# Conditioning sums moved between VectorE and GpSimd, and score matmuls in another order, in a one-core decoder layer

## The reference, cut to what matters

```
mod = silu(c) @ W_ada + b_ada          # 1024 x 6144: shift/scale/gate for both halves
h   = rms_norm(x) * (1 + scale1) + shift1
proj = h @ w_in                        # attention q,k,v; deltanet q,k,v; beta, decay; gates
branch A: window-128 attention, 8 query heads, 2 key heads, head width 64, sinks
branch B: gated delta rule, 4 heads of 128, short causal convolution on its inputs
x   = x + gate1 * ((sigmoid(gA)*(oA @ W_A) + sigmoid(gB)*(oB @ W_B)) @ w_out)
h   = rms_norm(x) * (1 + scale2) + shift2
x   = x + gate2 * ((silu(h @ w_gate) * (h @ w_up)) @ w_down)
```

## Time and profile before

| | us |
|---|---|
| median of 3 runs | 3558.05 (3557.0 to 3559.01) |
| the profiled execution | 3557.41 |
| its span, first to last instruction | 3555.7 |
| busy in the span: TensorE, VectorE, ScalarE, GpSimd | 3389.5, 1803.5, 1180.2, 176.1 |

### The profile page before, as it was taken

One profiled execution on the slowest core, in us unless ns is written; L12 is line 12 of the kernel. 1 busy time (PEld: TensorE's weight loads), 2 busy tenths in 40 slices (PEclk: granted clock), 3 DMA queues, 4 the chain that ended last, 5 costly groups with the idle time before them and its releaser, 6 DMA issues.

```text
span 3555.7 us, 49320 instructions
## 1 busy us (share of the span) xinstructions
PE 3389.5 (95%) x20664; PEld 2970.6 (84%) x20664; DVE 1803.5 (51%) x2806; ACT 1180.2 (33%) x1827; POOL 176.1 (5%) x171
## 2 busy tenths in 40 slices
PE   7999998999999999899999999899999999989999
PEld 7887788889888778798889777889888877788898
DVE  2866564434455565444354565544436465643333
ACT  1343343222233333323233334332223433432222
POOL 2001101000000100100000100000000010010000
PEclk9999999999999999999999999999999999989999
DMA  5430122332331113232232011322323211122222
GB/s 209 173 122 32 36 85 82 101 107 95 125 99 50 33 34 110 81 103 98 97 131 95 31 36 41 109 95 101 101 95 125 77 37 36 59 96 95 95 95 95
DMA packets 87388, 312.65 MB, mean 88 GB/s; under 512 B 10112, under 2 KB 18432, under 8 KB 85504
## 3 DMA queue, kind: packets, MB, share of 16 engines
q1 hardware_dynamic: 78720, 301.12, 25.1%
q10 hardware_dynamic: 8448, 8.39, 0.7%
HBM read 301.09 MB, written 8.39 MB: 87 GB/s over the span
## 4 chain that ended last, share of the span: by engine, by line
PE 85%; DVE 8%; ACT 3%; issue 1%; POOL 1%; DVEq 1%; POOLq 0%; ACTq 0%
PE gb L1306 37%; PE gb L1323 26%; PE gb L1562 5%; PE mb L1516 3%; PE mb L1499 2%; PE gb L1356 2%; PE gb L1251 2%; PE mb L1434 1%; PE mb L1273 1%; POOL d_rs L518 1%; PE mb L1504 1%; PE mb L1459 1%; DVE conv_acc L983 1%; PE mb L1519 1%; DVE d_ss L1085 1%
## 5 line engine op out<-in xcount | busy, mean ns | idle before, releaser
L570 ACT ACTIVATE w_hi<-w_raw 128x1024 fp32r<-128x1024 f32 x492 | 520.3, 1058 | 1258.7 <-PE gb L1306 601.8
L1306 PE MATMUL gb<-h_hi,w_hi 128*128 128x512 f32 x2256 | 891.5, 395 | 2.1 <-DVE w_lo L863 2.1
L863 DVE TENSOR_TENSOR w_lo<-w_raw,w_hi 128x1024 fp32r<-128x1024 f32 x492 | 600.5, 1222 | 576.0 <-ACT w_hi L570 571.3
L1306 PE MATMUL gb<-h_hi,w_lo 128*128 128x512 f32 x2256 | 887.1, 393 | 0.0
L1306 PE MATMUL gb<-h_lo,w_hi 128*128 128x512 f32 x2256 | 883.6, 392 | 0.0
L1306 PEld LDWEIGHTS gb<-h_hi,w_hi 128*128 128x128 f32 x2256 | 424.2, 188 | 87.2 <-DVE w_lo L863 4.2
L1306 PEld LDWEIGHTS gb<-h_hi,w_lo 128*128 128x128 f32 x2256 | 424.1, 188 | 85.1
L1306 PEld LDWEIGHTS gb<-h_lo,w_hi 128*128 128x128 f32 x2256 | 424.1, 188 | 84.7
L1323 PE MATMUL gb<-w_hi,hid_lo 128*128 128x256 f32 x1408 | 398.5, 283 | 0.0
L1323 PE MATMUL gb<-w_lo,hid_hi 128*128 128x256 f32 x1408 | 398.5, 283 | 0.0
L1323 PE MATMUL gb<-w_hi,hid_hi 128*128 128x256 f32 x1408 | 398.4, 283 | 0.0
(11 more groups left out here) (274 smaller groups left out, 4829.3 us busy)
## 6 DMA issues: line engine op xcount, KB each, us to landing
w_raw<-in_wstream SPq DMA_DIRECT2D x492, 512.0 KB, 3.3
ada_buf<-in_ada_w SPq DMA_DIRECT2D x12, 2048.0 KB, 8.0
xs<-in_x SPq DMA_DIRECT2D x16, 512.0 KB, 4.5
x<-in_x SPq DMA_DIRECT2D x4, 2048.0 KB, 8.6
out<-x ACTq DMA_DIRECT2D x16, 512.0 KB, 4.8
bias_row<-in_ada_br SPq DMA_DIRECT2D x1, 1024.0 KB, 11.9
gains<-in_qkg SPq DMA_DIRECT2D x1, 64.0 KB, 12.0
nrm_g<-in_g SPq DMA_DIRECT2D x2, 4.0 KB, 3.8
```

The costliest lines, as they stand in the source:

```text
L570: act.activation(w_hi[s][:, :], w_raw[s][:, :], ACT.Copy).then_inc(w_high.sem, 1)
L863: dve.tensor_tensor(w_lo[s][:, :], w_raw[s][:, :], w_hi[s][:, :].bitcast(fp32), ALU.subtract).then_inc(w_ready.sem, 1)
L1306: last = pe.matmul(bank(j), w, r, start=(i == 0), stop=(i == n - 1))
```

## The change

1. The first four turns go to VectorE (`ada_sums(0..3)`), between the scalings of the first four token tiles. TensorE makes only the sum over partitions. Turns 0 to 3 have buffers of their own, loaded first; the token rows `xs` of tiles 0 and 1 come behind turn 0, turn 3 comes in two halves.
2. Turns 4 to 9 go to GpSimd: it multiplies the whole 128x4096 piece by the vector, then adds halves (2048, 1024 and 512 elements a partition). They stand in its program directly behind the four shifts of the rows.
3. Turns 10 and 11 stay on VectorE, turn 10 behind the small chain on beta and decay, turn 11 in the output gate; they use a fifth buffer. TensorE takes the turns in the order 4, 5, 6, 7, 8, 10, 9, 11. SyncE loads turn 6, 7, 8, 9 ahead of units 9, 12, 15, 18.
4. The angles of the rotary embedding (some 22 small VectorE operations) and the `w_lo` of units 0 and 1 move from VectorE's start to behind the last `h_lo`.
5. The score matmuls alternate between the two halves of the rows, and the products of the probabilities with the values are issued own-own-old-old instead of own-old-own-old.

The core of the diff:

```diff
-ADA_ISSUE = {0: (4, 5), 8: (6,), 11: (7,), 14: (8,), 17: (9,), 20: (10,), 22: (11,)}
+ADA_ISSUE = {0: (4, 5), 4: (10,), 9: (6,), 12: (7,), 15: (8,), 18: (9,), 20: (11,)}
+ADA_ORDER = (0, 1, 2, 3, 4, 5, 6, 7, 8, 10, 9, 11)
+ADA_ON_POOL = (4, 5, 6, 7, 8, 9)
...
+            pool.wait_ge(c_silu, 1)
+            for turn in ADA_ON_POOL:
+                buf = ada_buf[turn % 2]
+                pool.wait_ge(ada_in[turn % 2], 16 * (turn // 2))
+                pool.tensor_tensor(buf[:, :, :], buf[:, :, :], cs[:, :].unsqueeze(2).to_broadcast([P, KD, 512]), ALU.mult)
+                for n in (4, 2):
+                    pool.drain()
+                    pool.tensor_tensor(buf[:, 0:n, :], buf[:, 0:n, :], buf[:, n:2 * n, :], ALU.add)
+                pool.drain()
+                pool.wait_ge(ada_prod, ada_place(turn - 2))
+                pool.tensor_tensor(ada_total(turn), buf[:, 0, :], buf[:, 1, :], ALU.add).then_inc(ada_pooled, 1)
...
-            for t in range(NT):
-                scale_tile(t)
-            split(0, 0)
-            split(0, 1)
             dve.wait_ge(cond_in, 16 * N_COND)
             dve.wait_ge(c_silu, 1)
-            for early in range(ADA_FIRST):
-                modulation(early)
+            ada_sums(0)
+            scale_tile(0)
+            scale_tile(1)
+            ada_sums(1)
+            modulation(0)
+            scale_tile(2)
+            ada_sums(2)
+            modulation(1)
+            scale_tile(3)
+            ada_sums(3)
+            modulation(2)
+            modulation(3)
...
+            norm_low(2, 3, h_hi, h_lo)
+            norm_low(3, 4, h_hi, h_lo)
+            split(0, 0)
+            split(0, 1)
             dve.wait_ge(pos_in, 16)
...
-                    if b == 0 and c in (2, 5, 8, 11):
-                        ada_sums(ADA_FIRST + c // 3)
-                    if b == 0 and c in (9, 11):
-                        modulation(4 + (c - 9) // 2)
+                    if b == 0 and c in (8, 11):
+                        modulation(4 + (c - 8) // 3)
...
-                        for parity in range(2):
-                            rows = slice(64 * parity, 64 * parity + 64)
-                            for old, keys in enumerate((kT[t % 2], kT[(t + 1) % 2])):
-                                for a in range(2):
+                        for old, keys in enumerate((kT[t % 2], kT[(t + 1) % 2])):
+                            for a in range(2):
+                                for parity in range(2):
+                                    rows = slice(64 * parity, 64 * parity + 64)
                                     last = pe.matmul(m(2 * g + parity)[:, 2 * old + a, :], qT[rows, 2 * g + a, :],
                                                      keys[rows, g, :], start=True, stop=True)
```

More of the change, by code:

```diff
@@ L421, in _, with load_piece @@
             sp.dma_start(nrm_g[:, 1, :], g2).then_inc(cond_in, 16)
-            for turn in range(2):
-                sp.dma_start(ada_buf[turn][:, :, :], ada_w[turn]).then_inc(ada_in[turn], 16)
+            def load_piece(turn, k, some=slice(0, KD)):
+                sp.dma_start(ada_buf[k][:, some, :], ada_w[turn][:, some, :]).then_inc(ada_in[k], 16)
+            load_piece(0, 0)
+            for i in range(2):
+                sp.dma_start(xs[:, i, :], x_t[0, :, i, :]).then_inc(xs_loaded[i].sem, 16)
+            load_piece(1, 1)
+            load_piece(2, 2)
+            load_piece(3, 3, slice(0, 4))
+            load_piece(3, 3, slice(4, 8))
             for i in (2, 3):
@@ L426, in _ @@
                 sp.dma_start(xs[:, i % 2, :], x_t[0, :, i, :]).then_inc(xs_loaded[i % 2].sem, 16)
-            for turn in range(2, ADA_FIRST):
-                sp.dma_start(ada_buf[turn][:, :, :], ada_w[turn]).then_inc(ada_in[turn], 16)
+            sp.dma_start(pos_i[:, :], pos).then_inc(pos_in, 16)
             def load_unit(b, u):
@@ L796, in _ @@
             MAGIC = float(1.5 * 2 ** 23)
[L797 to L820, removed]
             def modulation(turn):
                 v, half = divmod(turn, 2)
-                dve.wait_ge(ada_prod, turn + 1)
+                dve.wait_ge(ada_prod, ada_place(turn))
                 if is_gate(turn):
@@ L919, in _ @@
             norm_low(3, 4, h_hi, h_lo)
+            split(0, 0)
+            split(0, 1)
+            dve.wait_ge(pos_in, 16)
+            dve.tensor_copy(pos_f[:, :], pos_i[:, :])
+            dve.drain()
+            for f in range(HALF):
+                dve.tensor_scalar(ang[:, :, f], pos_f[:, :], float(freq[f]), None, ALU.mult)
+            dve.drain()
+            for quarter, dst in ((0.0, ang_r), (0.25, ang)):
+                dve.tensor_scalar(turn[:, :, :], ang[:, :, :], 1.0 / TWO_PI, quarter, ALU.mult, ALU.add)
+                dve.drain()
+                dve.tensor_scalar(turn[:, :, :], turn[:, :, :], MAGIC, None, ALU.add)
+                dve.drain()
+                dve.tensor_scalar(turn[:, :, :], turn[:, :, :], MAGIC, None, ALU.subtract)
+                dve.drain()
+                src = ang
+                for part in (T1, T2, T3):
+                    dve.scalar_tensor_tensor(dst[:, :, :], turn[:, :, :], -part, src[:, :, :], ALU.mult, ALU.add)
+                    dve.drain()
+                    src = dst
+                if quarter:
+                    dve.tensor_scalar(dst[:, :, :], dst[:, :, :], float(np.pi / 2), None, ALU.add)
+                    dve.drain()
+                dve.tensor_scalar(dst[:, :, :], dst[:, :, :], 3.1415925, -3.1415925, ALU.min, ALU.max
+                                  ).then_inc(ang_done, 1)
+                dve.drain()
             dve.wait_ge(consts_in, 16 * N_CONSTS)
@@ L1244, in _, with ada_product @@
             pe.wait_ge(c_silu, 1)
[L1246 to L1261, removed]
+            def ada_product(turn):
+                k = ADA_ORDER.index(turn)
+                if turn in ADA_ON_POOL:
+                    pe.wait_ge(ada_pooled, turn - ADA_FIRST + 1)
+                else:
+                    pe.wait_ge(ada_done, turn + 1 if turn < ADA_FIRST else ADA_FIRST + turn - 9)
+                if k >= ADA_FIRST + 2:
+                    pe.wait_ge(ada_read, k - 1)
+                total = ada_total(turn)
                 if is_gate(turn):
@@ L1275, in norm_turn @@
                 last.then_inc(n_turn.sem, 1)
+            ada_product(0)
             norm_turn(0, 1)
             norm_turn(1, 2)
-            for turn in range(ADA_FIRST):
-                ada_first(turn)
+            for turn in range(1, ADA_FIRST):
+                ada_product(turn)
             for t in (2, 3):
@@ L1448, in _, with values @@
                                  else v_prev[:, 64 * g:64 * g + 64])
-                        for odd in range(2):
+                        def values(odd, v, part):
                             o_ap = m(3)[64 * odd:64 * odd + 64, 2 * g:2 * g + 2, :]
-                            pe.matmul(o_ap, v_own, pT[g][0][:, odd::2, :], start=True, stop=False)
-                            last = pe.matmul(o_ap, v_old, pT[g][1][:, odd::2, :], start=False, stop=True)
+                            return pe.matmul(o_ap, v, pT[g][part][:, odd::2, :], start=(part == 0), stop=(part == 1))
+                        values(0, v_own, 0)
+                        values(1, v_own, 0)
+                        values(0, v_old, 1)
+                        last = values(1, v_old, 1)
                     last.then_inc(attn_out.sem, 1)
```

82 lines of the change are left out of this document (45 added, 37 removed).

## The result

The changed kernel takes 3574.86 us (median of 5 runs, 3572.87 to 3578.12) against 3557.0 us before (3556.5 to 3559.01): ratio 1.005, 95% interval 1.0035 to 1.0065. It is slower by 0.5%. (The table ahead of the prediction has 3558.05 for the kernel before, from three of the five.) The profiled execution took 3573.24 us, its span is 3571.5 us.

A forecast was written before the change was run, and what follows sets the result against it. Bound: early conditioning's chain of waits, VectorE and TensorE about balanced, then TensorE after 200 us. Profiled 3557.4 + 45.5 (later first scores) - 17.9 (score groups) = 3585 us; range 3535 to 3604, the forecast's own 3568 to 3600.

The forecast's parts named there:

- The early turns: Start, first four turns on VectorE: last product ends at 48.6 us instead of 74.84, 26.2 us earlier; last shift at 62.0.
- One engine waits for the whole operation of the other: Last shift to unit 17: VectorE and GpSimd wait for each other's whole instruction, so their times add up.
- GpSimd 14.1 us a turn, 84.4 in all, all of it lost: Turns 4 to 9 on GpSimd: 14.1 us each against VectorE's 6.26, six turns 84.4 us, added to VectorE's 81.0.
- the dearer price: Turns on GpSimd: the skill's 4497 ns for adding 2048 fp32 elements, making six turns 101 us, the sum 17 us more.
- Unit 17 ready at 234.4, 2 us for the clock: End of the convolutions: TensorE starts unit 17 43.5 us late, plus 2 for the clock's restart: +45.5 to first scores.
- TensorE's waits for `w_lo`: Sign that the forecast is right: these waits total over 40 us between 60 and 240 us.
- The scores, 0.56 us for each of 32 groups: Alternated score matmuls: 13 steps fall to 8 a group, 17.9 us less in all; the values gain nothing.
- The sum: Whole kernel: 3557.4 + 45.5 - 17.9 = 3585.0 us, slower by 0.8%.
- GpSimd beside VectorE: Rival for turns 4 to 9: GpSimd runs beside VectorE without holding it up; 3518 us, faster; chance 0.17.
- Half hidden: Rival for turns 4 to 9: GpSimd needs the port half its time, 42 of 84.4 us go; 3543 us; chance 0.10.
- Alternation without gain: Rival for the scores: a matmul's two passes must follow each other, so alternating brings nothing; 3603 us; chance 0.10.
- The crossing point: Border between faster and slower: 57 us of GpSimd time that VectorE loses.

The follow-up runs named there:

- pool_half: The changed kernel with half of each GpSimd turn left out (2048 elements multiplied, one addition of 1024, one of 512); 3529.2 us.
- pool_least: The changed kernel with each GpSimd turn cut to its last addition of 512 elements, all loads, waits, products and orders kept; 3510.3 us.
- no_alternation: The changed kernel with the scores and the values in the order of before; 3596.1 us.
- pool_pieces: The changed kernel with the same GpSimd work cut into operations of 512 elements; 3559.7 us.

## Why the prediction was right

Forecast 3585 us, slower with 0.70; measured 3574.9 (18 us over before instead of 28). The mechanism was the right one, and pool_half and pool_least show it by itself. By its steps:

- *The early turns.* The last product was to end at 48.6 and ended at 48.29; the last shift was to end at 62.0 and ended at 61.24. Right.
- *One engine waits for the whole operation of the other.* Right, now for operations four times as long as the trace of before had: 8.04 us for a `w_lo` behind a multiplication. This is what the Trainium skill says (SBUF — State Buffer, SBUF: two separate sides), and the trace agrees, even for a copy of three elements (4.56 us).
- *GpSimd 14.1 us a turn, 84.4 in all, all of it lost.* The total was nearly right, 80.1, by two errors against each other. A turn is 15.2 us of operations: the rate of the earlier trace rows, whose second operand is a broadcast one, holds for the multiplication (7.02 against 7.5) but not for the additions of two tensors, 4.62 us for 2048 elements instead of 3.75. Here the dearer price that the prediction had set aside is right: the Trainium skill (GPSIMD Engine Reference, 3.1 Elementwise) has 4497 ns for it. Against that, some 11 of the 91 us (6 x 15.2) didn't fall on VectorE: for 3.8 us of GpSimd's turns it was idle, and some of its operations don't wait (last section); the rest isn't split up. That the total came out is luck.
- *Unit 17 ready at 234.4, 2 us for the clock.* It was 231.8. The chunk behind it took 13.05 us instead of 11.62, 1.4 us for the clock. First scores 277 predicted, 273.6 measured: 3.1 us too late. TensorE's waits for `w_lo` were to be over 40 us and were 61.6. The longest of them, 22.0 us for units 0 and 1 behind GpSimd's first turn, isn't named in the prediction, though its time is in the sum.
- *The scores, 0.56 us for each of 32 groups.* Measured 0.54 us, 17.2 in all; the values nothing. Right.
- *The sum.* Behind the first scores it took off 17.9 us; the profile has 26.6. 17.2 of them are the groups. The other 9.4 are the remaining matmuls, 10.2 us shorter with 59 us at 1.2 GHz against 93, less 0.8 us of idle time. For this the prediction had no term, and it could not have read one out of a single profile. With the 3.1 us of the start this is the distance to the profiled execution: 3585.0 - 3573.2 = 11.8, of which 3.1 + 8.7 are these two.
- *The rivals.* GpSimd beside VectorE (3518) is out by the rows; with GpSimd's work nearly taken away the kernel stands at 3510, so that price was 8 us too high. Half hidden (3543) is out too: VectorE lost 80.1 us, not 42. Alternation without gain (3603) is what no_alternation measures, 3596, and it is out. The crossing point was put at 57 us of VectorE's time; the runs put it at 63.

## What to carry to other kernels

An engine that looks idle in the profile isn't free if its operations shut the busy one out, as GpSimd's did here (8.04 us for a `w_lo` of 1.22): before moving elementwise work from VectorE to GpSimd, price it as if VectorE did it at GpSimd's pace (here 15.2 us of operations in place of 6.3, of which 80.1 / 6 = 13.4 were lost), and look in the trace for a pair of overlapping rows that shows it. If it must go there, cut it in pieces about as long as VectorE's own operations (here 15 us of 18 came back by the medians, 9 of 16 by the profiled executions). A change made of several parts should be timed in parts: this one held a start worth 25 us (with the moved operations put back) and an alternation worth 19 to 23, both hidden by a third part that cost more.

## What the runs showed of the hardware

The lock is not on every operation of VectorE. In GpSimd's last turn (multiplication from 207.59 to 214.61, additions from 214.75 on) VectorE's timeline reads:

```profile
208.54 0.18 DVE L1036 TENSOR_TENSOR g_a<-mb,dtb 128x16 f32<-128x16 f32 x1 [6.74 <-PE mb L1418]
210.03 4.61 DVE L1039 TENSOR_SCALAR g_e<-g_e 128x16 f32<-128x16 f32 x1 [1.31 <-ACT g_e L659]
214.71 0.25 DVE L1041 RECIPROCAL g_b<-g_e 128x16 f32<-128x16 f32 x1
215.04 4.36 DVE L1043 TENSOR_SCALAR g_nb<-g_b 128x16 f32<-128x16 f32 x1
```

A tensor_tensor with one operand in PSUM (`mb`) runs in 0.18 us in the middle of the multiplication; a tensor_scalar of 16 elements from SBUF waits 4.6 us for it to end, although it has a single tensor operand. The prediction had counted only operations with two operands in SBUF as locked.

GpSimd's price depends on the operand: 7.02 us / 4096 = 1.71 ns an element with a broadcast operand (a multiplication), 4.62 / 2048 = 2.26 ns with two tensors (an addition). At 1024 elements both are additions: 1.90 us with a broadcast operand, 2.34 with two tensors.

In these profiles the record of the granted clock starts only with the first stretch at full clock (at 88.7 us before, 72.6 in pool_pieces). Ahead of it the clock column reads 1.00, whatever the pace: count matmuls there (the earlier trace rows has 18 and then 34 in 3.9 us).
